# Two-layer hybrid decoder step: four PSUM slots, fewer VectorE operations and another order of tiles in the RG-LRU stage

## The reference, cut to what matters

```
h = rmsnorm(x);  q, k, v, g_ret, x_lru, y_lru, g_a, g_b = split(h @ w_in)
ret_branch = (silu(g_ret) * groupnorm(retention(q, k, v, S))) @ w_ret_out
xc, new_buf = causal_conv(x_lru, conv_buf, conv_w, conv_b)       # 4 taps
r, i = sigmoid(blockdiag(xc, w_a) + b_a), sigmoid(blockdiag(xc, w_x) + b_x)
log_a = -8 * r * softplus(-lam);  a = exp(log_a)
u = sqrt(-expm1(2 * log_a)) * (i * xc);  h_t = a_t * h_(t-1) + u_t
lru_branch = (gelu(y_lru) * h_lru) @ w_lru_out
x += (sigmoid(g_a + b0) * ret_branch + sigmoid(g_b + b1) * lru_branch) @ w_o
x += (silu(gate) * up) @ w_down                                   # of rmsnorm(x)
```

## Time and profile before

| | us |
|---|---|
| median of three runs | 2627.15 |
| the profiled execution, its own time | 2625.86 |
| its span, first to last instruction | 2623.6 |
| TensorE busy | 2475.0 (94%) |
| VectorE busy | 1369.9 (52%) |
| ScalarE busy | 592.1 (23%) |
| GpSimd busy | 1411.0 (54%) |
| granted TensorE clock over the span | 0.977 |

### The profile page before, as it was taken

The page is one execution under the profiler, slowest core; times in us unless marked ns, Lnnn a source line. Parts: engine busy times, 40 slices in busy tenths (PEclk is TensorE's granted clock), DMA queues, the critical chain, the costliest instruction groups (busy, mean ns, idle before and its releaser), DMA issues.

```text
span 2623.6 us, 51666 instructions
## 1 busy us (share of the span) xinstructions
PE 2475.0 (94%) x19604; PEld 2408.0 (92%) x19604; DVE 1369.9 (52%) x1719; ACT 592.1 (23%) x849; POOL 1411.0 (54%) x845
## 2 busy tenths in 40 slices
PE   7999999978999999999999999998889998999997
PEld 7899999877989999999998999998879998999997
DVE  6565555588564643133255555647785646330333
ACT  2312222144341111001113222131525311100111
POOL 4354545444556656666653545544445665666664
PEclk9999999989999999999999999999889999999998
DMA  4454645312222222222245635452212222223222
GB/s 163 161 183 158 200 147 178 111 55 67 81 80 91 87 81 91 93 88 89 96 129 188 202 141 177 144 183 85 64 62 84 88 93 81 88 84 96 93 81 88
DMA packets 113008, 298.42 MB, mean 114 GB/s; under 512 B 11680, under 2 KB 12448, under 8 KB 112864
## 3 DMA queue, kind: packets, MB, share of 16 engines
q1 hardware_dynamic: 60480, 199.78, 23.2%
q10 hardware_dynamic: 52384, 96.56, 10.7%
HBM read 255.92 MB, written 40.38 MB: 113 GB/s over the span
## 4 chain that ended last, share of the span: by engine, by line
PE 78%; DVE 10%; DVEq 6%; issue 2%; ACT 1%; ACTq 1%; DMA 1%; POOL 0%; POOLq 0%
PE proj L322 71%; DVEq L1118 2%; DVE scratch L930 2%; PE aux L492 2%; PE aux L454 1%; DVE scratch L1020 1%; PE aux L508 1%; PE aux L484 1%; DVE scratch L1024 1%; DVEq L929 1%; DVE scratch L794 1%; ACTq L1440 1%; PE aux L471 1%; DVE scratch L995 0%; DVE residual L1109 0%
## 5 line engine op out<-in xcount | busy, mean ns | idle before, releaser
L308 POOL TENSOR_SCALAR w_high<-w_raw 128x1024 fp32r<-128x1024 f32 (+3 forms) x420 | 443.0, 1055 | 1126.4 <-PE proj L322 1102.3
L310 POOL TENSOR_TENSOR w_low<-w_raw,w_high 128x1024 fp32r<-128x1024 f32 (+3 forms) x420 | 967.6, 2304 | 62.1 <-issue 1.2
L322 PE MATMUL proj<-x_high,w_high 128*128 128x260 f32 x4096 | 845.6, 288 | 79.0 <-DVE scratch L1002 33.6
L322 PE MATMUL proj<-x_high,w_low 128*128 128x260 f32 x4096 | 834.3, 286 | 0.0
L322 PE MATMUL proj<-x_low,w_high 128*128 128x260 f32 x4096 | 832.8, 285 | 0.0
L322 PEld LDWEIGHTS proj<-x_high,w_high 128*128 128x128 f32 x4096 | 641.8, 192 | 96.9 <-issue 45.0
L322 PE MATMUL proj<-split_scratch,w_high 128*128 128x260 f32 x4000 | 656.9, 287 | 44.3 <-DVE scratch L903 16.8
L322 PEld LDWEIGHTS proj<-x_low,w_high 128*128 128x128 f32 x4096 | 640.4, 191 | 0.0
L322 PEld LDWEIGHTS proj<-x_high,w_low 128*128 128x128 f32 x4096 | 640.4, 191 | 0.0
L322 PEld LDWEIGHTS proj<-split_scratch,w_high 128*128 128x128 f32 x4000 | 557.9, 192 | 50.1 <-DVE scratch L903 18.0
L322 PE MATMUL proj<-split_scratch,w_low 128*128 128x260 f32 x2000 | 407.5, 286 | 0.0
(11 more groups left out here) (153 smaller groups left out, 1885.2 us busy)
## 6 DMA issues: line engine op xcount, KB each, us to landing
w_raw<-in_wstream SPq DMA_DIRECT2D x252, 512.0 KB, 3.3
scratch<-in_sret ACTq DMA_DIRECT2D x64, 512.0 KB, 6.7
out_ret_s<-scratch ACTq DMA_DIRECT2D x64, 512.0 KB, 4.8
w_raw<-in_wstream SPq DMA_DIRECT2D x72, 448.0 KB, 3.2
w_raw<-in_wstream SPq DMA_DIRECT2D x48, 384.0 KB, 3.0
scratch<-v_rows ACTq DMA_DIRECT2D x64, 256.0 KB, 4.4
w_raw<-in_wstream SPq DMA_DIRECT2D x48, 320.0 KB, 2.7
out_ret_p<-scratch ACTq DMA_DIRECT2D x8, 512.0 KB, 2.8
```

Of the source, the lines that this page charges most:

```text
L308: pool.tensor_scalar(WH[:, j, w], WR[:, j, w], 1.0, 0.0, ALU.mult, ALU.add)
L310: pool.tensor_tensor(WL[:, j, w], WR[:, j, w], WH[:, j, w].bitcast(F32), ALU.subtract).then_inc(s["w_split"], 1)
L322: m = pe.matmul(out, wt[:, w, blk * P:(blk + 1) * P], x[xi], start=first and n == 0, stop=last and n == 2)
```

## The change

Between the last head's output projection and the merge, projection tiles use four slots: the eight banks are one tensor, slots 2 and 3 being the banks that the retention has done with. A table (`SLOT`, `BEFORE`) tells TensorE which earlier tile has to be read before a tile may start. The order is a list (`LRU_ORDER`): for each t a y tile with gates of group 0, the x tile t of group 1, and the merge gate A tile t; then y tile 0 of group 1, gate A tile 5, the eight LRU output tiles, the other four y tiles of group 1, and gate A tiles 6 and 7. The merge turns keep gate B and the LRU output (8 and 5 blocks). Weight units follow that order; their number stays the same.

VectorE no longer scales r: the factor goes into ScalarE's exponential and tanh, and ScalarE makes a second exponential in place of VectorE's square of a. In the convolution three small operations for the samples become one, from a sum made once a layer (`conv_of_states`), and three copies become one; ScalarE's DMAs then store the pieces. The softplus series (`decays`) moves into the first head of the layer, behind v tile 2, and `conv_of_states` behind v tile 3. In the first head ScalarE makes products 4 and 5 and the last two silus ahead of the next state loads, and VectorE two of the last four state updates earlier, with the second sample product between the two final-state products on TensorE.

The core of the diff:

```diff
+X_EARLY = 4
+
+
+LRU_ORDER = ([("x", 0, t) for t in range(X_EARLY, GT)]
+             + [w for t in range(GT) for w in (("y", 0, t), ("x", 1, t), ("ga", 0, t))]
+             + [("y", 1, 0), ("ga", 0, GT)] + [("out", 0, m) for m in range(MT)]
+             + [("y", 1, t) for t in range(1, GT)] + [("ga", 0, m) for m in range(GT + 1, MT)])
+LRU_UNITS = tuple(n for k, _, t in LRU_ORDER
+                  for n in {"x": (MT,), "y": (YG_UNIT[t % GT],) * 2, "ga": (MT,), "out": (GT,)}[k])
+
+MERGE = ((MT + GT + 1) // 2, (MT + GT) // 2)
...
+C_RING = C_RET
+SLOT = {i: (TILE0 + i) % 2 for i in range(C_RING - 2, C_RING)}
+SLOT |= {i: (TILE0 + i - C_RING) % 4 for i in range(C_RING, C_MERGE)}
+assert SLOT[C_MERGE - 1] != (TILE0 + C_MERGE) % 2
+
+BEFORE = {i: max([k for k in SLOT if k < i and SLOT[k] == SLOT[i]], default=None) for i in SLOT}
...
-        PP = ctx.enter_context(nc.psum_tensor("proj", [P, 2, 2, 512], F32))
-        AUX = ctx.enter_context(nc.psum_tensor("aux", [P, 4, 512], F32))
+        BANKS = ctx.enter_context(nc.psum_tensor("banks", [P, 8, 512], F32))
+        PP = BANKS[:, :, :].rearrange("p (s c) n -> p s c n", c=2)
+        AUX = BANKS[:, 4:8, :]
...
             def tile_begin(tb, idx):
-                pe.wait_ge(s["t_free"], tb + (idx - 1))
+                if C_RING <= idx < C_MERGE:
+                    if BEFORE[idx] is not None:
+                        pe.wait_ge(s["t_free"], tb + (BEFORE[idx] + 1))
+                else:
+                    pe.wait_ge(s["t_free"], tb + (idx - 1))
...
-                    for d in range(KT):
-                        final_state(d)
+                    final_state(0)
                     if first:
                         sample_out(1)
+                    final_state(1)
...
                 for t in range(X_EARLY, GT):
                     x_tile(0, t)
-                y_gates(0)
                 for t in range(GT):
+                    y_gates(0, t)
                     x_tile(1, t)
+                    gate_a(t)
+                y_gates(1, 0)
+                gate_a(GT)
                 pe.wait_ge(s["gl_low"], layer * LT + GT)
-                pe.sem_inc(s["go_pe"], 1)
+                for m_ in range(MT):
+                    lru_out(ub0, B_OUT[m_], tb0, C_OUT[m_])
+                for t in range(1, GT):
+                    y_gates(1, t)
+                for m_ in range(GT + 1, MT):
+                    gate_a(m_)
...
+                def decays():
...
+                    for n in range(17, 0, -2):
+                        tt(acc, acc, z2, ALU.mult)
+                        dve.drain()
+                        ts(acc, acc, 1.0 / n, None, ALU.add)
+                        dve.drain()
...
+                def conv_of_states():
+
+                    for j in range(CW - 1):
+                        w = CUR[:, PC_CW:PC_CW + LT * CW].rearrange("p (c j) -> p c j", j=CW)[:, :, j:j + 1]
+                        part = SCS if j == 0 else SCT
+                        dve.drain()
+                        if j == 0:
+                            dve.wait_ge(s["state_ld"], layer * 32 + 32)
+                        tt(part[:], SCV[:, :, j, :], w.broadcast_to([P, LT, NS]), ALU.mult)
+                        if j:
+                            dve.drain()
+                            tt(SCS[:], SCS[:], SCT[:], ALU.add)
...
                         v_tile(e)
+                        if first:
+                            (decays if e == 2 else conv_of_states)()
...
-                    dve.tensor_copy(CVP[:, c, :], xr[:, SEQ - CW + 1:SEQ])
-                    dve.tensor_copy(CVS[:, c, 0:CW - 2, :], SCV[:, c, 1:CW - 1, :])
-                    dve.tensor_copy(CVS[:, c, CW - 2, :], xr[:, SEQ:TOK])
+                    dve.tensor_copy(XT[:, c, :], xr[:, SEQ - CW + 1:TOK])
                     for j in range(CW - 1):
                         d = CW - 1 - j
                         dve.drain()
-                        stt(XCF[:, t, d:SEQ], xr[:, 0:SEQ - d], cw(j), XCF[:, t, d:SEQ],
-                            ALU.mult, ALU.add)
-                        m = stt(XCF[:, t, SEQ:TOK], SCV[:, c, j, :], cw(j), XCF[:, t, SEQ:TOK],
+                        if j == 0:
+                            tt(XCF[:, t, SEQ:TOK], XCF[:, t, SEQ:TOK], SCS[:, c, :], ALU.add)
+                        m = stt(XCF[:, t, d:SEQ], xr[:, 0:SEQ - d], cw(j), XCF[:, t, d:SEQ],
                                 ALU.mult, ALU.add)
                     m.then_inc(s["xc_full"], 1)
 
...
                 def use_gates(g, t):
 
-                    b, c = t % 2, g * GT + t
-                    dve.wait_ge(s["gate_r"], layer * LT + (c + 1))
-                    ts(LA[:, b, :], LA[:, b, :], CUR[:, PC_SP + c:PC_SP + c + 1], None, ALU.mult
-                       ).then_inc(s["t_free"], 1)
+                    c = g * GT + t
+
                     dve.wait_ge(s["gate_i"], layer * LT + (c + 1))
-                    tt(IX[:, b, :], IX[:, b, :], XCF[:, t, :], ALU.mult).then_inc(s["t_free"], 1)
-
-                def one_less_a2(g, t):
-
-                    b = t % 2
-                    dve.drain()
-                    dve.wait_ge(s["th_full"], layer * LT + (g * GT + t + 1))
-                    tt(DF, AF[:, b, :], AF[:, b, :], ALU.mult)
-                    dve.drain()
-                    stt(DF, DF, 1.0, LA[:, b, :], ALU.add, ALU.mult).then_inc(s["d_full"], 1)
-
-                def scan(g, t):
-
-                    b, c = t % 2, g * GT + t
+                    tt(IX[:, c % 2, :], IX[:, c % 2, :], XCF[:, t, :], ALU.mult).then_inc(s["t_free"], 1)
+                    dve.drain().then_inc(s["t_free"], 1)
+
+                def one_less_a2(c):
+
+                    b = c % 2
+                    dve.drain()
+                    dve.wait_ge(s["th_full"], layer * LT + (c + 1))
+                    stt(DF[b], DF[b], 1.0, LA[:, b, :], ALU.add, ALU.mult).then_inc(s["d_full"], 1)
+
+                def scan(c):
+
...
                         keep(3)
-                        silu(2)
-                        next_states()
                         product(4)
                         product(5)
+                        silu(2)
                         silu(3)
+                        next_states()
                     else:
...
+                def gates(g, t):
+                    c, idx = g * GT + t, C_Y[g][t]
+                    b = c % 2
+                    act.wait_ge(s["p_done"], tb0 + (idx + 2))
+                    A(halves(LA[:, b, :]), pp(idx + 1), ACT.Sigmoid,
+                      bias=CUR[:, PC_BA + c:PC_BA + c + 1])
+                    act.wait_ge(s["p_done"], tb0 + (idx + 3))
+                    A(halves(IX[:, b, :]), pp(idx + 2), ACT.Sigmoid,
+                      bias=CUR[:, PC_BX + c:PC_BX + c + 1]).then_inc(s["gate_i"], 1)
+                    act.drain()
+                    A(AF[:, b, :], LA[:, b, :], ACT.Exp, scale=NEG[:, c:c + 1])
+                    A(DF[b], LA[:, b, :], ACT.Exp, scale=NEG2[:, c:c + 1])
+                    act.drain()
+                    A(LA[:, b, :], LA[:, b, :], ACT.Tanh, scale=CUR[:, PC_SP + c:PC_SP + c + 1]
+                      ).then_inc(s["th_full"], 1)
+                    act.wait_ge(s["t_free"], tb0 + (idx + 1))
+                    A(YF[:, b, :], YF[:, b, :], ACT.Gelu_apprx_tanh).then_inc(s["y_gelu"], 1)
+
+                def root(c):
+                    act.wait_ge(s["d_full"], layer * LT + (c + 1))
+                    A(DF[c % 2], DF[c % 2], ACT.Sqrt).then_inc(s["w_sqrt"], 1)
+
+                def sig_ga(m_):
+                    act.wait_ge(s["t_free"], tb0 + (C_GA[m_] + 1))
+                    A(GB[m_], GB[m_], ACT.Sigmoid,
+                      bias=CUR[:, PC_BG + m_:PC_BG + m_ + 1]).then_inc(s["sg_m"], 1)
...
```

More of the change, by code:

```diff
@@ L209, in build @@
         SQT = fview(at["rt"], 2, TOK)
-        e_, z_, z2, acc = (DEC[:, LT * i:LT * (i + 1)] for i in range(4))
+        e_, z_, z2, acc = (SOFT[:, i, :] for i in range(4))
+        NEG, NEG2 = z_, z2
         ACCL = fview(0, MT, TOK)
@@ L891, in one_head @@
                            ).then_inc(s["o_norm"], 1)
-                    for n in range(SRING if first else SRING + 2, NS):
+                    for n in range(SRING + 2, NS):
                         new_state(n)
@@ L1408, in _ @@
-                conv_high(1, 0)
-                gated_high(0, GT - 1)
-                for t in range(1, GT):
-                    conv_high(1, t)
-                y_gates(1)
-                gated_high(1, GT - 1)
+                for t in range(GT):
+                    gates(0, t)
+                    if t:
+                        conv_high(1, t - 1)
+                        gated_high(t - 1)
+                    root(t)
+                    sig_ga(t)
+                gates(1, 0)
+                conv_high(1, GT - 1)
@@ L1414, in _ @@
+                gated_high(GT - 1)
+                root(GT)
+                sig_ga(GT)
+                for t in range(1, GT):
+                    gates(1, t)
+                    gated_high(GT + t - 1)
```

(21 more changed lines are left out.)

327 lines of the change are left out of this document (152 added, 175 removed).

## The result

The changed kernel takes 2577.86 us (median of four runs, 2575.09 to 2584.28), the kernel before 2626.46 on the same chip: ratio 0.9818, 95% interval 0.9801 to 0.9835. That is 48.6 us (1.8%) faster. The sign was right, the size was half: 92 us had been forecast, and the result lies 3 us above the range.

A forecast was written before the change was run, and what follows sets the result against it. PSUM slot waits and half clock were taken to lose 122.7 us in the LRU stages over both layers; 30.2 would stay, so 2625.9 - 92.5 + 0.7 for first heads = 2534 us (2535 against the median), range 2512 to 2575.

The forecast's parts named there:

- All are waits for a PSUM slot: LRU stage before: TensorE's waits of 16.8, 12.7 and 6.7 us are for PSUM slots, not for operands.
- I take 1.5 us a unit: Group 0 turns: GpSimd's disturbance of VectorE per weight unit, four units a turn, making the turn 18.4 us.
- The undisturbed sum of 12.4 us: Group 0: VectorE's work in one turn without disturbance from GpSimd, 12.4 us.
- TensorE does not wait: Group 0: VectorE's 18.4 us turn stays inside TensorE's 20.2 or 21.6 us, so no wait.
- The first rival: LRU stage: GpSimd makes VectorE the bound above 2.1 us a unit; total 2600 us; chance 0.08.
- It falls back about 1 us per pair: Output projection: VectorE lags 4 us over eight tiles, which the two extra slots (5.8 us) take up.
- (a) LRU output: Before the LRU output tiles: wait 2.9 us, up to 5 with disturbance, and 1.7 us of clock.
- (b) First merge tile: Before the first merge tile: slot read behind the last scan; wait 7.5 us (4.5 to 10), 1.7 of clock.
- the slower rival: Everywhere, each GpSimd operation stops VectorE whole; 71 us lost against 61, heads 12 more; about 2655 us; chance 0.02.
- The wait behind the series: First head: softplus series delays v tile 3, so sample transposes wait some 4 us; with clock 5.7 lost.
- I get 4.8 us back in layer 0: First head: earlier ScalarE products and state updates shorten waits before the fourth attention group and next head; 5.9 in layer 1.
- That rival: Second group: ScalarE's table switches each stop it 1.4 us longer and bound it; 2569 us; chance 0.04.

The follow-up runs named there:

- the subtraction short: Kernel before, with GpSimd's subtraction on 64 of a weight unit's columns and the rest of the low part left out: 2517.9 us, ratio 0.9577.
- the short subtraction: Changed kernel, with GpSimd's subtraction on 64 of a weight unit's columns and the rest of the low part left out: 2486.1 us, ratio 0.9447.
- the series cut in two: Changed kernel, with three of the softplus series' nine steps behind v tile 2 and the rest behind the last gate tile's read: 2563.2 us, ratio 0.9748.

## Why the prediction was half right

**What bounds the kernel before.** The stage, the 122.7 us lost in it and the waits were read rightly. "All are waits for a PSUM slot" is true of the last link and hid the one below: with the subtraction short, 77 of the 122.7 us go without a slot added.

**Group 0: the step that failed.** "I take 1.5 us a unit, below the 1.9 lost in that row since not every unit meets such an operation." Nearly every unit does: 2.2 to 2.6 us in the two turns that cost most. The undisturbed sum of 12.4 us was right (24.15 less 10.3 of stops less 1.1 for ScalarE is 12.7; 1.1 us of waiting for the second gate had not been counted). With 1.1 and 2.3 the turn is 12.7 + 1.1 + 4 x 2.3 = 23 us, past TensorE's 20.2 and 21.6, so "TensorE does not wait" fell. It cost 13.6 us in layer 0 where nothing was forecast: 3.05, 1.11, 2.31 and 2.36 us of waits, and 4.8 of clock (a stretch of 6.8 us at half clock from 551.1, 0.6 of it idle, and one of 3.4). It takes both, the stops and a merge gate tile read last in the turn: with shorter stops, or with that read earlier, the last three waits go. The first rival, that VectorE becomes the bound at more than 2.1 us a unit, was the mechanism; it had 0.08. Its price of 2600 us took all 3.4 us of every unit.

**The output projection.** "It falls back about 1 us per pair" fell too: VectorE's stops from its start to 551.7 us came to 13 us over seven weight units, and the 3.05 us, with 3.1 of the clock, belong here.

**(a) LRU output.** 2.3 and 2.6 us with 1.7 of clock against 2.9 and 1.7: right.

**(b) First merge tile.** 9.1 and 7.5 us against 7.5 (4.5 to 10). The cause is right: the slot is read behind the last scan, and reading it earlier takes the wait away. That the size agrees owes something to luck. ScalarE was to set the pace with turns of 10.9 us; in layer 0 they took 14.8, 11.2 and 13.3, of which it waited 5.8 us for VectorE:

```profile
728.12 0.64 ACT L1473 ACTIVATE scratch<-scratch 128x520 f32<-128x520 f32 x1 [1.37 <-DVE scratch L1067]
...
749.83 0.64 ACT L1451 ACTIVATE split_scratch<-scratch 128x520 fp32r<-128x520 f32 x1 [1.78 <-DVE scratch L1083]
...
755.19 0.69 ACT L1460 ACTIVATE scratch<-banks,params_cur 128x520 f32<-128x520 f32 x1
```

VectorE's own stops between 712 and 770 us came to 14.8 us. So the last sigmoid ended 9.7 us behind the last gate tile (746.2 to 755.9), where 4.5 had been reckoned. The chain behind it took 13.4 us in place of 14.5, and TensorE came 2.6 us later itself, 2.0 of them a second slot wait that was not seen (the last y tile, read behind a scan): that left 9.1. With 1.8 us of clock the two waits cost 12.9 against 9.2, and with the short subtraction 5.3 us are left of the first and nothing of the second.

**Sum for layer 0.** 13.6 + 4.0 + 12.9 and 1.9 for joints are the 32.4 us above 302.9; 15.1 had been forecast. (In the slower rival the terms 25, 20, 9 and 15 make 69 a layer, not 71; its 2655 goes with 69.)

**First head.** The wait behind the series (3.1 with 1.7 of clock) was forecast as 4 with 1.7, and the one before the fourth group as 0.8; it is 0.59. What failed is "I get 4.8 us back in layer 0". The state loads now come later, and a wait of 1.58 us for one appears; the next head's 2.74 us fell by 0.6 only. And two stretches of 3.4 us at half clock, from 35.7 and 141.5 us, cost 1.7 us each: they stand behind gaps of 1.9 and 2.2 us, while the same two gaps in the kernel before (1.8 and 2.7 us) had none behind them. Why the clock fell there only now stays open. Layer 0 lost 4.7 us up to the stage and layer 1 1.3. Another 3.5 us went behind the merge, over both layers. Half clock lasts 6.8 us there, 3.4 in the kernel before, with the same wait of 3.0 us ahead of it, which is some 3.0 of the 3.5:

```profile
906.10:912.93 6.83, 6.03 (x24) 5.65 (x25) 2.61 (x3) 3.06 (x4) 1.91 (x2) 0.50 0.01 2
```

**ScalarE.** No drain around table loads showed: from the start of a load to the next operation is 1.30 us (753.30 to 754.60), as the rows of before had said. That rival had no part; ScalarE's turns grew by waiting for VectorE.

## What to carry to other kernels

Where GpSimd and VectorE both work from SBUF for long and VectorE hardly idles, charge VectorE most of GpSimd's time (here 2.2 to 2.6 of some 3.5 us a unit in two turns, 1.7 in a third), not an average over lucky cases: a rival whose threshold (2.1 us) lies just above a guessed value (1.5) deserves far more than 0.08. A wait for a slot names the instruction that freed it; ask next why that one was late, before pricing more slots. And where one engine just keeps pace, put the reads that free slots ahead of its other work: that alone gave 17 us.

## What the runs showed that was not expected

GpSimd's stops fall on one kind of VectorE instruction only. Of 608 with an operand in PSUM none lasted 0.1 us longer than the shortest of its line and shape, in any of these traces; of the other 1,005 in the changed kernel 343 did, 349.5 us in all (before: 314 of 1,111, 292.3 us; short subtraction: 140, 49.5 us). The Trainium skill, "SBUF — State Buffer", section "Who interferes with whom", says that a VectorE instruction with at most one SBUF input, outside its two-port modes, does not contend with GpSimd; these counts agree for the ones that read PSUM. The change removed VectorE instructions and yet raised their stopped time by 57 us.

Gaps of the same length may be followed by half clock (1.2 GHz) for different times. Behind 3.0 us of waiting ahead of the feed-forward stage it lasted 3.4 us in the kernel before and 6.8 in the changed one, in both layers (some 1.5 and 3.0 us lost, as the stretch begins inside the gap); with the series cut in two it lasted 6.8 us in layer 0 and 3.4 in layer 1.
